# Two transformer layers and a hybrid layer on one core: the mixers' input tiles are multiplied with the unnormed x

## The reference, cut to what matters

```python
for l in range(2):
    mod = silu(c) @ ada_w[l] + ada_b[l]
    (sh1, sc1, g1, sh2, sc2, g2, sh3, sc3, g3) = split(mod, 9)
    h = rms_norm(x, ffn1_norm[l]) * (1 + sc1) + sh1
    x = x + 0.5 * g1 * ((silu(h @ w_gate) * (h @ w_up)) @ w_down)     # 1024 -> 2816 -> 1024
    h = rms_norm(x, mix_norm[l]) * (1 + sc2) + sh2
    z = h @ w_in[l]                                                  # 1024 -> 1216
    y = concat(causal_pool(z[:512]), latent_attention(z[512:]))      # q latent 384, kv latent 256, 64 rope
    x = x + g2 * (y @ w_out[l])
    h = rms_norm(x, ffn2_norm[l]) * (1 + sc3) + sh3
    x = x + 0.5 * g3 * ((silu(h @ w_gate) * (h @ w_up)) @ w_down)
x = rms_norm(x, final_norm)
# then the hybrid layer: state-space and attention mixer, and a fifth FFN
```

## Time and profile before

| | |
|---|---|
| median of 3 runs | 1251.11 us (1250.73 to 1252.66) |
| profiled execution | 1256.0 us, its span 1254.1 us |
| PE busy | 1236.2 us, 99% |
| DVE busy | 1010.8 us, 81% |
| ACT busy | 612.1 us, 49% |
| POOL busy | 126.8 us, 10% |
| granted clock of TensorE | 0.996 |

### The profile page before, as it was taken

The page is one execution under the profiler, slowest core; times in us unless marked ns, Lnnn a source line. Parts: engine busy times, 40 slices in busy tenths (PEclk is TensorE's granted clock), DMA queues, the critical chain, the costliest instruction groups (busy, mean ns, idle before and its releaser), DMA issues.

```text
span 1254.1 us, 27223 instructions
## 1 busy us (share of the span) xinstructions
PE 1236.2 (99%) x11579; PEld 1208.5 (96%) x11579; DVE 1010.8 (81%) x1660; ACT 612.1 (49%) x890; POOL 126.8 (10%) x207
## 2 busy tenths in 40 slices
PE   9999999999999999999999999999999999999997
PEld 7999999999999999999999999999999988999997
DVE  4899998787988668999988889899975858766665
ACT  4543444577434647443336685433354476544333
POOL 0111110004111044111110012000001000000000
PEclk9999999999999999999999999999998999999999
DMA  9999998453788653999994435545542532555550
GB/s 368 394 404 385 360 364 329 135 160 110 286 337 334 235 196 132 347 377 354 360 378 160 153 117 192 213 154 196 211 149 86 161 144 84 201 203 201 189 181 36
DMA packets 66105, 293.96 MB, mean 234 GB/s; under 512 B 7744, under 2 KB 8896, under 8 KB 51904
## 3 DMA queue, kind: packets, MB, share of 16 engines
q1 hardware_dynamic: 47552, 225.10, 50.2%
q0 software_dynamic: 18432, 67.12, 13.4%
HBM read 291.14 MB, written 1.05 MB: 233 GB/s over the span
## 4 chain that ended last, share of the span: by engine, by line
PE 89%; DVE 6%; ACT 2%; issue 1%; DMA 1%; SPq 0%; DVEq 0%; ACTq 0%
PE gu_bank L702 17%; PE gu_bank L704 16%; PE gu_bank L703 16%; PE y_bank L702 7%; PE y_bank L704 7%; PE y_bank L703 7%; PE t_bank L702 3%; PE t_bank L704 3%; PE t_bank L703 3%; DVE dn_lo L1953 1%; PE y_bank L728 1%; PE y_bank L1176 1%; PE gu_bank L754 1%; PE y_bank L1267 1%; DMA pro<-ada 1%
## 5 line engine op out<-in xcount | busy, mean ns | idle before, releaser
L702 PE MATMUL gu_bank<-hT_hi,gu_hi 128*128 128x256 f32 x1656 | 458.3, 277 | 1.8 <-DVE gu_lo L1966 0.9
L704 PE MATMUL gu_bank<-hT_hi,gu_lo 128*128 128x256 f32 x1656 | 457.7, 276 | 0.0
L703 PE MATMUL gu_bank<-hT_lo,gu_hi 128*128 128x256 f32 x1656 | 457.7, 276 | 0.0
L702 PEld LDWEIGHTS gu_bank<-hT_hi,gu_hi 128*128 128x128 f32 x1656 | 310.8, 188 | 2.4 <-DVE gu_lo L1966 1.2
L704 PEld LDWEIGHTS gu_bank<-hT_hi,gu_lo 128*128 128x128 f32 x1656 | 310.9, 188 | 0.0
L703 PEld LDWEIGHTS gu_bank<-hT_lo,gu_hi 128*128 128x128 f32 x1656 | 310.8, 188 | 0.1
L1958 DVE TENSOR_TENSOR gu_lo<-raw_gu,gu_hi 128x2048 fp32r<-128x2048 f32 x103 | 236.1, 2292 | 31.8 <-ACT gu_hi L1451 29.2
L1451 ACT ACTIVATE gu_hi<-raw_gu 128x2048 fp32r<-128x2048 f32 x100 | 191.0, 1910 | 35.5 <-DMA raw_gu<-ffn_gu 35.4
L1472 ACT ACTIVATE sg<-gu_bank 128x256 f32<-128x256 f32 x82 | 31.6, 385 | 348.4 <-PE gu_bank L704 348.4
L702 PE MATMUL y_bank<-act_hi,dn_hi 128*128 128x256 f32 x660 | 183.5, 278 | 0.6 <-DVE act_lo L2017 0.6
L703 PE MATMUL y_bank<-act_lo,dn_hi 128*128 128x256 f32 x660 | 182.6, 277 | 0.0
(11 more groups left out here) (555 smaller groups left out, 2227.4 us busy)
## 6 DMA issues: line engine op xcount, KB each, us to landing
raw_gu<-ffn_gu SPq DMA_DIRECT2D x110, 1024.0 KB, 7.2
stage<-ada POOLq DMA_DIRECT2D x128, 512.0 KB, 8.0
raw_dn<-ffn_dn SPq DMA_DIRECT2D x110, 512.0 KB, 4.1
ring<-mix_w SPq DMA_DIRECT2D x72, 512.0 KB, 3.8
stage<-ada SPq DMA_DIRECT2D x8, 512.0 KB, 14.3
pro<-ada SPq DMA_DIRECT2D x6, 512.0 KB, 12.9
x<-x_in SPq DMA_DIRECT2D x1, 1024.0 KB, 5.6
ring<-ada SPq DMA_DIRECT2D x2, 512.0 KB, 17.5
```

Of the source, the lines that this page charges most:

```text
L702: pe.matmul(to, a[0], b[0], start=start, stop=False)
L703: pe.matmul(to, a[0], b[1], start=False, stop=False)
L704: return pe.matmul(to, a[1], b[0], start=False, stop=stop)
```

## The change

1. **Mixers raw.** `raw_halves` and `raw_residual` now also run ahead of the mixers, into `mix_raw_hi` and `mix_raw_lo`. PE multiplies tiles 0 and 1 chunk by chunk right after the FFN, then sums the squares, then starts tile 2, with `rows` in its middle. Every one of the ten tiles is multiplied by `rstdT` on DVE (`z_scale`), which also sums the two shift columns into `z_bias`; ACT squares and copies from SBUF with that bias. Gone are `sums`, `normed`, `partial`, `squares` of the mixers, and `busy`.
2. **POOL.** `raw_norm` serves kt = 1 to 5 and adds the squares of chunks 4 to 7 to those of 0 to 3 (one 128x1024 addition), so that PE sums four chunks: 64 small products where an FFN had 128 and a mixer 96. `raw_sums` waits for that addition; in an FFN it stands behind block 0's last chunk, no longer ahead of it, and `rows` two chunks later.
3. **Columns.** The shift's low part goes into the second extra column of `raw_hi`; the low pass has 256 columns. Sums of the two columns take the place of copies of one.
4. **FFN.** Two `shifted_lo` move from ahead of `raw_product(1)` to the other six.
5. **The start.** In `second_gate` the high weights' passes of chunks 0 to 6 come first, and the passes with the low half of the weights after them, behind its wait.
6. **DVE's list in the mixer** is interleaved anew with the ten `z_scale`.

```diff
@@ gpsimd
-            def raw_norm(r):
+            def raw_norm(kt):
                 for c in range(KC):
...
                     pool.tensor_tensor(sq_x[:, c, :], x[:, c, :], x[:, c, :], ALU.mult).then_inc(sq_done, 1)
-                pool.wait_ge(rows_copied, r + 1)
+                pool.wait_ge(sq_done, KC * kt + KC)
+                pool.tensor_tensor(sq_x[:, 0:4, :], sq_x[:, 0:4, :], sq_x[:, 4:8, :], ALU.add).then_inc(part_done, 1)
+                if kt % 3 == 1:
+                    return
+                pool.wait_ge(rows_copied, kt)
@@ tensor
             def raw_sums(kt):
                 to = ss_bank(kt)
-                pe.wait_ge(sq_done, KC * kt + KC)
+                pe.wait_ge(part_done, kt)
                 clear_rows(to)
-                for c in range(KC):
-                    last = token_columns(to, c, ones[:, 0:2], c == KC - 1)
+                for c in range(4):
+                    last = token_columns(to, c, ones[:, 0:2], c == 3)
...
+            def raw_product(kt, to, w, c):
+                hi = raw_hi_of(kt)[:, c, 0:S + 2]
+                pe.matmul(to[:, 0:S + 2], w[0], hi, start=c == 0, stop=False)
+                pe.matmul(to[:, 0:S], w[0], raw_lo(kt, c), start=False, stop=False)
+                return pe.matmul(to[:, 0:S + 2], w[1], hi, start=False, stop=c == KC - 1)
...
-                tiles = [(tile_bank()[:, 0:S], split_unit(l, n)) for n in range(3)]
-                by_chunk(3 * l + 1, [(to, lambda c, w=w: [a[:, tok(c)] for a in w], True, True, tile_ps) for to, w in tiles])
-                for n in range(3, ZT):
+                tiles = [(tile_bank(), split_unit(l, n)) for n in range(2)]
+                kt = 3 * l + 1
+                for c in range(KC):
+                    pe.wait_ge(raw_lo_done, raw_lo_at(kt) + c + 2)
+                    for to, w in tiles:
+                        last = raw_product(kt, to, [a[:, tok(c)] for a in w], c)
...
+                raw_sums(kt)
+                for n in range(2, ZT):
                     z_tile(n)
...
+            def second_gate():
+                pe.wait_ge(gu1_hi_half, 1)
+                for c in range(KC - 1):
+                    pe.wait_ge(hT_lo_done, c + 1)
+                    for a in (hT_hi, hT_lo):
+                        pe.matmul(gu_bank[1][:, 0:S], gu_hi[:, 1, 0, c, :], a[:, c, :], start=False, stop=False)
+                pe.wait_ge(gu1_lo_half, 1)
+                for c in range(KC - 1):
+                    pe.matmul(gu_bank[1][:, 0:S], gu_lo[:, 1, 0, c, :], hT_hi[:, c, :], start=False, stop=False)
@@ scalar, after each first FFN of a layer
                 split(l, 2)
                 table(ACT.Sqrt)
-                squares(3 * l + 1)
+                raw_halves(3 * l + 1)
+                split(l, SLOTS)
                 root(3 * l + 1)
-                shifted(3 * l + 1)
...
+                    act.wait_ge(z_scaled, ZT * l + n + 1)
+                    to, bias = z_home(n), z_bias[:, n:n + 1]
                     if n < QCH + KVCH:
+                        act.activation(sq[:, n, :], to, ACT.Square, bias=bias).then_inc(sq_ready, 1)
+                    act.activation(to, to, ACT.Identity, bias=bias).then_inc(tile_out, 1)
@@ vector
+            def raw_residual(kt):
+                k, hi = kt - 1, raw_hi_of(kt)
+                dve.wait_ge(raw_hi_done, raw_hi_at(kt) + 1)
...
+                def z_scale(n):
+                    dve.wait_ge(tile_ps, base + n + 1)
+                    dve.reduce_sum(z_bias[:, n:n + 1], zb[n % 4][:, S:S + 2], axis=AX.X)
+                    dve.tensor_tensor(z_home(n), zb[n % 4][:, 0:S], rstdT[:, :], ALU.mult).then_inc(z_scaled, 1)
...
                 split(l, 1, 1)
-                residual(3 * l)
+                raw_residual(3 * l + 1)
                 split(l, 2, 2)
-                normed(3 * l + 1)
                 gate(l, 1)
```

More of the change, by code:

```diff
@@ L437, in program @@
         NORMS = 3 * DEPTH
[L438 to L442, removed]
+        RAW_SCALED = 4 * (NFFN - 2)
+        HT_TOK = ht_at(NORMS) + KC
         Y_TOK = KC * NORMS
@@ L585, in _ @@
                 if q == PRO + 48 + STAGES:
[L586 removed]
+                    raw_norm(1)
+                    raw_norm(2)
                 if q in (PRO, PRO + STAGES // 2):
@@ L816, in gate_up_raw @@
                         for c in range(KC):
-                            if h == 0 and c == 2:
-                                rows(RAW[r])
-                            last = raw_part(r, 1, h, c)
+                            if h == 0 and c == 4:
+                                rows(kt)
+                            last = raw_part(kt, 1, h, c)
                     last.then_inc(gu_ps, 1)
@@ L894, in rows_of_tokens @@
                     last = pe.matmul(tb[0][:, tok(t)], rstd[:, t:t + 1].to_broadcast([P, P]), ident, start=True, stop=True)
-                last.then_inc(last_rows, 1)
+                last.then_inc(norm_rows, 1)
             def tokens_back(c):
@@ L917, in z_tile @@
                 def z_tile(n):
-                    product(tile_bank()[:, 0:S], split_unit(l, n)).then_inc(tile_ps, 1)
+                    to, w = tile_bank(), split_unit(l, n)
+                    for c in range(KC):
+                        if n == 2 and c == 4:
+                            rows(kt)
+                        last = raw_product(kt, to, [a[:, tok(c)] for a in w], c)
+                    last.then_inc(tile_ps, 1)
                 def mean_square(a, chunks):
@@ L1098, in _ @@
             clear(gu_bank[1])
-            second_products(0, range(KC - 1))
+            second_gate()
             first_products(KC - 1)
@@ L1104, in _ @@
                 ffn(2 * l, l > 0)
-                sums_after_ffn(2 * l)
+                pe.wait_ge(prod_done, FB * (2 * l + 1))
                 pe.wait_ge(masks_loaded, 16)
-                busy(1)
-                rows(3 * l + 1)
-                busy(2)
                 mixer(l)
@@ L1908, in shifted_lo @@
             def shifted_lo(kt, c):
-                dve.wait_ge(hT_hi_done, KC * kt + c + 1)
+                dve.wait_ge(hT_hi_done, ht_at(kt) + c + 1)
                 dve.scalar_tensor_tensor(hT_lo[:, c, :], hT[:, c, :], mods[:, KC + c:KC + c + 1], hT_hi[:, c, :].bitcast(F32), ALU.add, ALU.subtract)\
                    .then_inc(hT_lo_done, 1)
-            def normed(kt):
-                root(kt)
-                dve.wait_ge(norm_rows, kt)
-                for c in range(KC):
-                    scaled(kt, c, rows_ps)
-                    if c:
-                        shifted_lo(kt, c - 1)
-                shifted_lo(kt, KC - 1)
             def tok_norm(t):
@@ L2040, in ffn @@
                 if raw:
-                    kt = RAW[f - 1]
-                    root(kt)
+                    norm_root(kt)
                 split_dn(1)
                 if raw:
-                    dve.wait_ge(norm_rows, kt)
-                    dve.tensor_copy(rstdT[:, :], rows_ps).then_inc(rows_copied, 1)
-                    dve.wait_ge(rows_copied, f)
+                    raw_rows(kt)
                     raw_product(0)
                     halves(0)
-                    for c in range(2):
-                        shifted_lo(kt, c)
                     raw_product(1)
@@ L2060, in ffn @@
                     if raw and n == 0:
-                        for c in range(2, KC):
+                        for c in range(KC):
                             shifted_lo(kt, c)
@@ L2449, in _ @@
             first_sums()
-            root(0)
+            norm_root(0)
             first_chunk(0)
```

196 lines of the change are left out of this document (100 added, 96 removed).

## The result

The changed kernel takes 1296.31 us (median of 6 runs, 1295.55 to 1299.68), the kernel before 1254.52 (6 runs). The ratio is 1.034 (1.032 to 1.036): 42 us slower, where 0.5 us more than 1251.11 were forecast and 1253.9 was the upper end.

The account below looks back on a forecast made before the run. PE, busy 99%, was taken as the bound, with DVE ending last in the mixers. Mixers +1.8, FFN starts -1.35 and start 0 gave +0.45 us, so 1251.5 us; 8-in-10 range 1247.6 to 1253.9.

Parts of the forecast that it names:

- the three rivals: Whole kernel: front end's gain lasts, 1247.0 us (chance 0.26); DVE takes ports first, 1253.7 (0.16); start's microsecond stays, 1250.5 (0.05).
- the slower rival: Mixer front end: DVE's low half takes the ports before POOL's addition; +1.6 us per mixer, +2.6 in all, 1253.7; chance 0.16.
- The mixers: Both mixers: 1.2 us gained by tile 2's end, but DVE's list makes each end 0.9 us later, +1.8 together.
- 221.0: Mixer 0's front end: the time tile 2 begins, after PE waits 1.0 us for POOL and 0.8 for clearing and products.
- The addition: Mixer front end: POOL's 128x1024 addition of squares, taken as 2.15 us, between 1.2 and 2.44.
- The FFN starts: FFNs at kt = 2, 3, 5: fewer small products, less a wait for POOL's addition; 0.45 us gained each, -1.35 together.
- The start: Program start: the new order saves about 1 us, which becomes waiting for a weight transfer; worth 0, at most -1.0.
- The tile stage: Mixers from tile 4 to unit 12: DVE runs nearly without a break, its 5.1 us idle eaten up; unit 12's half 0.9 us later.

Follow-up runs that it names:

- before_shift64: The kernel before with 64 unused bytes where the change puts z_bias, nothing else changed: 1296.91 us, ratio 1.036 to the kernel before.
- after_same_places: The changed kernel with z_bias in unused space above the mixer's tiles, every old tile at its old address: 1254.49 us, ratio 1.0008 to the kernel before.
- top_eight_root: Changed kernel, old tiles at old addresses, mixers' sums over eight chunks without POOL's addition, root(0) and latent(0) earlier in DVE's list: 1250.59 us, ratio 0.9990.
- before_act128: The kernel before with the activations of the down products 128 bytes higher, both distances 64: 1282.26 us, ratio 1.022 to the kernel before.

## Why the prediction was wrong

**The step that failed** is the one that I took for granted: that only work and waiting taken off PE, or put on it, can move the time, so that an instruction which the diff leaves alone keeps its duration. The list of the change's parts has no line for a new 40-byte tile. It had the largest price of all: by the medians about 41 of the 42 us, shown by before_shift64 (1.036 with no other change) and after_same_places (1.0008 with all of the change but the place). None of the three rivals held it, and the range of 6.3 us was made of terms that all lie in the moved work.

**The moved work cost more than forecast, within the range.** +0.45 us was the sum; 1.0 (-0.5 to 2.5) by the medians and 2.3 at the same clock is what after_same_places measured. That is nearer to the slower rival's +2.6, but not by its cause: POOL came first, at 216.80, and DVE's low half behind it, at 216.92. By its terms, in the two profiled executions:

- *The mixers*: +0.9 each was forecast. Mixer 0 took 49.99 us from the FFN's end to the values (212.44 to 262.43) against 48.85, +1.1; mixer 1 49.85 (664.86 to 714.71) against 48.11 (664.64 to 712.75), +1.7. The forecast had taken mixer 0's figures for both, and the kernel before was 0.7 us quicker in mixer 1. PE did not stall in the chunks and waited 1.00 us for POOL, as forecast. Tile 2 began 7.92 us behind the FFN's end (8.0 forecast); the 0.8 us that the prediction gives for clearing and products doesn't lead to its own 221.0, the measured 1.08 nearly does. The addition took 2.43 us, not 2.15. It held DVE's low half for its whole remaining length: 3.39 us for one of 1.22, 2.17 more. The section "Who interferes with whom" of the Trainium skill's page "SBUF — State Buffer" calls the shared port pair an exclusive lock and says that the order of issue decides who blocks. The trace agrees: the low half started 0.12 us behind the addition and ended 1.08 us after its end.
- *The FFN starts*: -0.45 each was forecast. From the raw products' start in the second FFN to the end of the third, the kernel before took 368.03 us (296.61 to 664.64) and after_same_places 367.69 (297.17 to 664.86): -0.17 each. The addition takes 2.50 us there and PE's wait ahead of the second down product grew from 0.19 to 0.4. The sign was right, the size less than half.
- *The start*: 0 was forecast, and the kernels with the new and the old start are not told apart (1253.8 and 1253.7 us at the same clock).
- *The tile stage*: that DVE's list would eat up its waits and then set the end is what top_eight_root bears out; reordering it gave back 1.1 us in mixer 0. That raw tiles would run at the slower pace in tiles 6 to 9 (0.5 us per mixer) has no term in the sum; in after_same_places part of it hides behind PE's wait of 1.45 us for unit 12.

**What stays open** is why a distance is good. The runs show a pace of 113.3 ns, one of 117.8 and one near 119.6 (distance 0 for both kinds), and others between at distances 32 and 224. They show that the pace of a pass doesn't hang on its own two tiles alone: gate passes at distance 64 run at 113.3 in the kernel before and at 117.7 in before_act128, where of the FFN's big tiles only the activations of the down passes moved. Within the kernel before, the second FFN's gate passes run at 117.8 up to 328.0, and from the down product that starts there on all are at the faster pace (87 and 90 passes in 10 us):

```profile
318.00:328.00 10.00, 10.00 (x87) 10.00 (x86) 9.86 (x12) 3.14 (x3) 1.14 (x2) 1.00 0.67 238
328.20:338.20 10.00, 10.00 (x90) 10.00 (x89) 8.65 (x13) 4.50 (x5) 1.47 (x3) 1.00 0.97 369
```

What sets a stretch at one pace or the other, and what in the chip the distance acts on, no run here shows.

## What to carry to other kernels

When the bound engine gets slower in rows that the diff doesn't touch, count its instructions per window before looking for waits, and compare the addresses of the tiles: a new small tile ahead of big ones can move them all. Where float32 passes stream at full pace, put new small tiles behind the large ones, or pad them so that the distances between activations and weights stay the same modulo 256 bytes. And judge a change only with that held fixed, and at the same granted clock: here the place of one tile turned a change that costs 0.1 to 0.2% into one that costs 3%.

## What the runs showed of the hardware that was not expected

- The pace of these 128x256 float32 passes depends on the distances of activation and weight tiles in a partition, modulo 256 bytes: 113.3 ns between starts at best (64 for gate and up, 192 for down), 119.6 with both at 0.
- The same addresses can give two paces: with distance 192 for both kinds of pass one execution ran its first FFN at 851 passes per 100 us and its second at 885.
- POOL's addition of 128x1024 took 2.43 to 2.50 us, and a DVE subtraction that met it ran 3.39 us in place of 1.22.
